# A two-block transformer on one core: the second block's prologues, attention order, weight slots and long-convolution loads, rearranged

## What is computed

```python
def second_block(x, c, ctx, ...):
    for layer in range(4):
        ...
        hx = rmsnorm(x, g_pre[layer]) * (1.0 + scale_x) + shift_x
        hc = rmsnorm(ctx, g_pre[layer]) * (1.0 + scale_c) + shift_c
        if kind == 0:
            yx, yc = mla_mixer(hx, hc, ...)
        elif kind == 1:
            yx, yc = swa_mixer(hx, hc, ...)
        else:
            yx, yc = hyena_mixer(hx, hc, ...)
        x = x + gate_x * rmsnorm(yx, g_post[layer])
        if with_ctx_out:
            ctx = ctx + gate_c * rmsnorm(yc, g_post[layer])
```

## Time and profile before

| | us |
|---|---|
| three runs, median (lowest to highest) | 3139.94 (3133.66 to 3140.37) |
| the profiled execution | 3137.42 |
| its span of instructions | 3135.6 |
| PE busy | 2908.2 (93%) |
| DVE busy | 1859.2 (59%) |
| ACT busy | 1151.2 (37%) |

### The profile page before, as it was taken

The page is one execution under the profiler, slowest core; times in us unless marked ns, Lnnn a source line. Parts: engine busy times, 40 slices in busy tenths (PEclk is TensorE's granted clock), DMA queues, the critical chain, the costliest instruction groups (busy, mean ns, idle before and its releaser), DMA issues.

```text
span 3135.6 us, 36002 instructions
## 1 busy us (share of the span) xinstructions
PE 2908.2 (93%) x14361; PEld 2337.9 (75%) x14361; DVE 1859.2 (59%) x3353; ACT 1151.2 (37%) x2022; POOL 94.2 (3%) x177
## 2 busy tenths in 40 slices
PE   7999889999999999999998888999998878989997
PEld 5767657778888887887787776888865556767885
DVE  5436677877676566663636566465436666455544
ACT  4224233232223444444534444443222110454443
POOL 0000000000000000000100000020000000000000
PEclk9999999999999999999999999999999998999999
DMA  6222115545554241103211110333331210321102
GB/s 236 88 88 91 52 59 201 201 175 181 169 168 134 94 141 61 58 24 101 81 50 31 31 31 4 128 116 101 106 92 34 64 53 25 125 77 58 41 18 94
DMA packets 109312, 288.77 MB, mean 92 GB/s; under 512 B 18326, under 2 KB 37815, under 8 KB 108888
## 3 DMA queue, kind: packets, MB, share of 16 engines
q1 hardware_dynamic: 97880, 249.05, 24.2%
q0 software_dynamic: 9392, 32.48, 2.8%
q10 hardware_dynamic: 1872, 4.93, 0.4%
HBM read 257.05 MB, written 24.12 MB: 90 GB/s over the span
## 4 chain that ended last, share of the span: by engine, by line
PE 81%; DVE 10%; ACT 5%; issue 1%; DMA 1%; SPq 1%; ACTq 0%; POOL 0%; DVEq 0%; POOLq 0%
PE ps L1826 19%; PE ps L1828 19%; PE ps L1827 19%; PE ps L2061 5%; PE ps L1859 2%; PE ps L2119 2%; PE ps L2093 2%; PE ps L2048 2%; ACT pt L2391 2%; PE ps L2135 1%; PE ps L1975 1%; PE ps L2082 1%; DVE tmp L2727 1%; PE ps L2016 1%; PE ps L2018 1%
## 5 line engine op out<-in xcount | busy, mean ns | idle before, releaser
L1826 PE MATMUL ps<-hh,whi 128*128 128x256 f32 (+1 forms) x2424 | 919.4, 379 | 24.6 <-DVE hl L2567 12.0
L1827 PE MATMUL ps<-hl,whi 128*128 128x256 f32 (+1 forms) x2424 | 871.8, 360 | 0.0
L1828 PE MATMUL ps<-hh,wlo 128*128 128x256 f32 (+1 forms) x2424 | 871.6, 360 | 0.0
L1826 PEld LDWEIGHTS ps<-hh,whi 128*128 128x128 f32 x2424 | 459.7, 190 | 130.6 <-issue 26.2
L1827 PEld LDWEIGHTS ps<-hl,whi 128*128 128x128 f32 x2424 | 460.5, 190 | 90.2 <-issue 21.2
L1828 PEld LDWEIGHTS ps<-hh,wlo 128*128 128x128 f32 x2424 | 459.0, 189 | 71.3
L2576 DVE TENSOR_TENSOR wlo<-raw,whi 128x1024 fp32r<-128x1024 f32 x249 | 303.9, 1222 | 243.8 <-ACT whi L2198 243.2
L2198 ACT ACTIVATE whi<-raw 128x1024 fp32r<-128x1024 f32 x249 | 262.4, 1055 | 300.9 <-PE ps L1828 274.5
L2061 PE MATMUL ps<-pt,v 128*128 128x256 f32 x768 | 215.8, 404 | 27.2 <-ACT pt L2391 16.1
L2391 ACT ACTIVATE pt<-ps 128x512 f32<-128x512 f32 (+1 forms) x200 | 109.5, 579 | 249.1 <-PE ps L2048 248.8
L2887 DVE TENSOR_REDUCE sm<-ps 128x1 f32<-128x768 f32 (+3 forms) x176 | 129.4, 735 | 93.1 <-PE ps L2018 48.4
(11 more groups left out here) (373 smaller groups left out, 4568.4 us busy)
## 6 DMA issues: line engine op xcount, KB each, us to landing
raw<-in_wall SPq DMA_DIRECT2D x249, 512.0 KB, 4.3
mb<-in_wmod SPq DMA_DIRECT2D x128, 512.0 KB, 3.6
xb<-xpark SPq DMA_DIRECT2D x24, 384.0 KB, 4.7
xpark<-F POOLq DMA_DIRECT2D x32, 256.0 KB, 2.3
upark<-tmp POOLq DMA_DIRECT2D x18, 384.0 KB, 2.7
u<-upark SPq DMA_DIRECT2D x24, 256.0 KB, 3.1
tmp<-tmp SPq DMA_DIRECT2D x80, 64.0 KB, 2.0
early<-in_wm SPq DMA_DIRECT2D x8, 512.0 KB, 6.4
```

The lines of the kernel that those rows point to most:

```text
L1826: e.matmul(out, L[0], R[0], start=start, stop=False)
L1827: e.matmul(out, L[0], R[1], start=False, stop=False)
L1828: return e.matmul(out, L[1], R[0], start=False, stop=stop)
```

## The change

The new code differs from the old in all of these places; the functions that are not named stay as they are. The first block is the same but for its end.

- **Layer 0**: `context_norm`, `square_sums` and `first_in` go. After the feed-forward network come `rms_stages` for the final norm, `final_gain`, the norm of all 768 columns (`layer_in`), and then three tiles together. Fourteen zero matmuls precede the first sums and 22 the first products.
- **MLA input**: the squares of the latents are taken in `latent_norm` itself, after the tiles before it are done, and the layout order of the weight blocks (`latent_tiles`) goes with `Two`.
- **Layer to layer**: `Two` holds three tiles on both sides instead of six, `XH`/`XL` and the slots' bookkeeping go, and 22 zeros stand before the first product of the next layer.
- **Attention**: the projections of the next head or tile are played in one go ahead of the present one's units, with banks by `take`; their evictions follow at once. Each row of scores claims two banks. One `bias` serves both rows. `rope` is four ACT copies of 32 partitions. SWA gets 17, 14 or 7 zeros ahead of a tile's first scores.
- **Long convolutions**: `load_u` moves from behind `conv_out` to the last frequency block of a transform, and the first inputs of the context line come behind four steps of the spectra.

```diff
-    XH, XL = (sb([P, NS, SLOT], F32R, x, sE) for x in ("xhi", "xlo"))
...
-    idle_before = {"out": 9, "head": 10}
+    idle_before = {2: 14, (11, NC_): 9, (12, NC_): 9, (13, NC_): 9, ("lat", 0, 0): 12, ("lat", 3, 0): 12, "out": 9, "head": 10,
+                   ("tile", True, 0): 17, ("tile", False, 0): 14, ("tile", False, 1): 7}
...
+    xf = [[(dve, ("ffn", 1, c))] for c in range(8)]
+    R = rms_stages(2, F, xf, NC_, T, D, KD)
+    for k in range(KD):
+        stage("final_gain", k, R, [R] if k == KD - 1 else [])
...
+        R = rms_stages(10 + l, F, tx, 0, T, D, KD)
+        h_done[l] = [(dve, ("H", 10 + l, KD - 1))]
+        return norm_stages(10 + l, tx, SEGS, (COEF[:, c + 8:c + 16], COEF[:, c:c + 8]),
+                           (MODC[:, c0:c0 + 8], MODX[:, c0:c0 + 8]), (dve, ("coef_in", l)), 0, R, (act, ("rstd", 10 + l)), hfree)
...
-        last = Two(6, 0, KD, H, src, src)
+        last = Two(3, KD, H, src, src, False)
...
         rest(0)
         bx = root(NC_, T)
-        stage("rstd", [root_of(NC_, T, bx)])
+        root_2(NC_, T, bx)
+        rest(1)
+        rest(2)
...
-                if u["w"] > 512:
-                    u["bk"].append((banks.claim(2 * s), banks.claim(2 * s + 1)))
-                else:
-                    u["bk"].append((banks.claim(2 * s + self.side[s]),))
-                    self.side[s] = 1 - self.side[s]
+                u["bk"].append((banks.claim(2 * s), banks.claim(2 * s + 1)))
                 stage("score", u, s, u["bk"][s], u["sm"])
-                stage("bias", u, s, u["sm"])
+            stage("bias", u, u["sm"])
...
-        play(tile_stages(KD, H, tH, gr, cq(3)))
-        squares = latent_squares(0, 4, gr)
-        play(tile_stages(KD, H, tH, SEGS, cq(4)))
-        latent_norm(0, 4, gr, 512, col("gq", 4 * j, 4), squares)
+        for c in (4, 5):
+            play(tile_stages(KD, H, tH, SEGS, cq(c)))
+        latent_norm(0, 4, gr, 512, col("gq", 4 * j, 4))
         play(tile_stages(KD, H, tH, SEGS, ev_kr))
-        latent_norm(4, 2, SEGS, 256, col("gkv", 2 * j, 2), squares)
+        latent_norm(4, 2, SEGS, 256, col("gkv", 2 * j, 2))
...
         for h in range(8):
+            if h + 1 < 8:
+                make_qk(h + 1)
+            if h % 2 and h < 6:
+                make_qr(h // 2 + 1)
+                make_v(h // 2 + 1)
             attend_head(h)
...
-        first = Two(6, 3, KD, H, sx, sc)
-        cross(before, l, first, evac, 6)
+        first = Two(3, KD, H, sx, sc, True, warm=[(None, 22)])
+        cross(before, l, first)
...
-                    if qt == 3 and tile < 7:
-                        make_q(tile + 1)
-                    if qt == 4 and tile % 2 == 0 and tile < 6:
-                        make_k(tile // 2 + 1)
...
         for tile in range(8):
+            if tile + 1 < 8:
+                make_q(tile + 1)
+            if tile % 2 == 0 and tile < 6:
+                make_k(tile // 2 + 1)
             attend_tile(tile)
...
                         stage("inverse", m, o, f - 1, seg, ib)
+                    if f == nt - 1:
+                        load_u(seg)
...
                     stage("z_out", l, m, a, n, q, s0)
                     ups[seg].drop(s0)
-                load_u(seg)
...
         stage("tables_in", 1)
         stage("tables_in", 0)
-        load_u(0)
...
         for _ in range(4):
             next(ahead)
+        load_u(0)
...
         def rope(g, b, src, cs, cs_mark, scale, swap, j, m, name):
-            wait_all(w, (pe, g), m)
-            A(TMP[:, m.i, 0:src.shape[1]], src, ACT.Copy).then_inc(*act.up(("rope", name), b))
+            n = src.shape[1]
+            wait_all(w, (pe, g), j)
+            for d, s, c in swap:
+                x = A(TMP[d:d + c, j.i, 0:n], src[s:s + c, :], ACT.Copy, scale=1.0 if scale is None else scale)
+            x.then_inc(*act.up(("rot", name)))
```

More of the change, by code:

```diff
@@ L291, in build_program @@
         tiles += [("long", 0), ("long", 1)] if x else [("short",)]
[L292 to L293 removed]
+    tiles += range(248, wall.shape[0])
+    wt = {"made": 0, "at": 0, "end": {}, "cap": len(tiles) - 1, "limit": len(tiles) - 1}
     plain, slot_free, last_h = set(), {}, []
[L297 removed]
     def block(tile, k, width=1):
         m = wt["at"] // 8
[L302 to L304 removed]
+        while wt["made"] <= min(m + AHEAD, wt["cap"]):
+            prepare()
         tile.blocks[k] = (m, (wt["at"] % 8) * P)
@@ L307, in block @@
         wt["at"] += width
[L309 to L327, removed]
-    def prepare(lows=True):
-        m = wt["made"]
-        if m not in plain:
-            s = next(x for x in slots if x[0] < NS or m < wt["six"])
-            slots.remove(s)
-            slot_of[m] = s
-        stage("weights", m)
+    def prepare(lows=True):
+        stage("weights", wt["made"])
         if lows:
-            stage("weights_lo", m)
+            stage("weights_lo", wt["made"])
         wt["made"] += 1
@@ L405, in step @@
             if k == 0:
-                g.banks = [banks.claim(i) for i in at] or [banks.take() for _ in range(tok // 2 if tok else len(groups))]
+                g.banks = [banks.take() for _ in range(tok // 2 if tok else len(groups))]
             block(g, k, 2 if tok else 1)
@@ L1027, in layer_out, with cross @@
         align()
-    def cross(before, l, first, leave, n):
+    def cross(before, l, first):
         tO, att_end = before
@@ L1058, in rest @@
             for k in range(KD):
-                last.context(i, k)
+                last.context(i, k, False)
         def root(a, b):
@@ L1274, in flush, with stacked @@
             self.multiply()
-    def stacked(g, i, dst, name, free, later, context=None):
+    def stacked(g, i, dst, name, free):
         a, b = g.groups[i]
@@ L1380, in mla @@
         tk = [(dve, ("half", l, 4 + k)) for k in range(2)]
-        wt["six"] = 0
-        free = [(dve, ("half", l, 6)), *att_free, *[(pe, ("w", m)) for m in slot_of if slot_of[m][0] >= NS]]
+        free = [(dve, ("half", l, 6)), *att_free]
         ptr = Ring(4)
@@ L1442, in attend_head @@
                               "ptfree": free, "vfree": v if h % 2 and end else None, "drops": [(vb, v)] if h % 2 and end else []})
-                    for _ in range(1 if with_ctx else 2 - i):
-                        next(between, None)
             qn.drop(b2["qn", h])
@@ L1792, in enter_3 @@
     def enter_3(gr, cq):
-        first = Two(3, 3, KD, H, *normed(3)[:2], False)
-        cross(before, 3, first, cq, 6)
+        first = Two(3, KD, H, *normed(3)[:2], True, warm=[(None, 22)])
+        cross(before, 3, first)
+        wt["cap"] = wt["limit"]
+        pump(3)
+        for c in range(3):
+            cq(c)(first.main_tiles[c])
         return normed(3)[2], None
```

611 lines of the change are left out of this document (175 added, 436 removed).

## The result

The new kernel takes 3357.63 us (3352.57 to 3358.74); the old one, run beside it on the same chip, 3140.15. The ratio is 1.069, 95% interval 1.067 to 1.071. The forecast was 3246 with a range of 3180 to 3335: right in direction, wrong in size. The change costs 217 us, twice the 106 of the sum.

A forecast was written before the change was run, and what follows sets the result against it. PE, busy 93% of the span, was taken as the bound, so each place was costed as PE time without a product; the terms summed to 106 us on 3137.4, giving 3246 against the runs' median, range 3180 to 3335.

The forecast's parts named there:

- the units stay PE's: MLA: 7.4 us of PE work in a 768-column unit against a softmax loop of 6.1, so PE's part is longer.
- +8 and +6: MLA of layers 0 and 3: uncovered units and waits behind `take` cost 8 and 6 us; ends 0 and 20 each.
- About 1 us: MLA: what the projections covered, the short context unit and a head's first unit, was about 1 us for each.
- DVE's modulation work: MLA of layer 0: this work ends before the stage in the new order and gives about half of 16 us back.
- +42: SWA: projections in front and the softmax loop cost 32 us, a lower clock 10 more; ends +10 and +90.
- +11.5, +11.5, +6.5: Three layer changes: 6.5 us each for lost cover, plus 5 at the first two for the context norm's wait.
- The chain gets shorter: Layer changes: three fewer DVE additions and a merged root save about 2 us, so 8.4 - 2 = 6.5 each.
- 5 us gap at the first context product: Layer changes: PE was to show a gap of about 5 us before the first context product.
- Layer 0's entry (+19): Between feed-forward network and first products: 31 us without products in the new order, less 12 before, costs 19 us.
- the latents (+6.5): MLA input: 12 zeros (2.8 us) and the last two sums' waits (3.7) cost 6.5 us, in layers 0 and 3.
- -8: Convolutions: moving the input loads frees waits for a filter's weights and a spectrum, 8 us gained; range -12 to +6.
- A cold PE in both kinds of attention: Rival: gaps lower PE's clock, all SWA units at 1.2 GHz and both MLA layers at +20: 3335 us; chance 0.23.

The follow-up runs named there:

- a_rows128: The new kernel with the remainder matmuls of all scores contracting 128 partitions again instead of 64: 3292.36 us, ratio 1.050 to the old kernel.
- b_swa_front: The old kernel with SWA's projections of the next tile played in one go in front of each tile, rotation still by DMAs: 3177.20 us, ratio 1.014.
- a_sum: The new kernel with 128-partition score remainders, no 22 zeros at the three layer changes, and the old order of squares and roots there: 3252.89 us, ratio 1.038.
- a_swa_cold: The new kernel with 128-partition score remainders and without the zeros ahead of a tile's first scores in SWA: 3294.56 us, ratio 1.050.

## Why the forecast was wrong, point by point

**The missing term: 61 us by the ratios.** The forecast went through the edits by name (order, banks, biases, rotation, zeros) and never through the matmuls' operands; "the units stay PE's" took PE's work as unchanged. It was the largest single cost of all: 17.0, 30.7 and 16.9 us in the new kernel's stretches, with 5.6 of the last a lower clock.

**MLA (+8 and +6; without the height 25.6 and 14.8).** Two steps failed. "About 1 us" for what the projections covered was 1.57 or more for the second unit alone, and the price stood in the old trace's last head. The waits behind `take`, put at 2 us for four heads, were 1.2 to 2.2 at six. Gross the gaps made 20.5 in layer 0 and not 16, and no row shows anything of the half that was credited to DVE's modulation work.

**SWA (+42; +49.4, of which 30.7 is the height).** The total looks right by two errors that cancel. The term for fronts and loop was 42 and is 18.7 in a_rows128. The loop did not grow as costed: with 128 partitions and ACT copies the new SWA, with its single bias, is 333.1 us against 331.2, although 16.8 us of products left it and 15.8 of zeros came. The eviction in front was sized well for DMAs (b_swa_front +43), but the change itself takes these DMAs away. The forecast costed the ACT copies, and what they spare only as an end of its range. (Its sum for that eviction is also off: the listed terms make 7.8 before any overlap, and it says 8.2 with it, some 3 us over seven tiles.) Its sign, some 375 us from first to last score, came true (357.1 and the 16.8 that were moved out), which shows that a total alone is a weak test.

**Layer changes (+11.5, +11.5, +6.5; measured 21.7, 19.4 and, less 8.1 for the latents, 21.2).** "The chain gets shorter" was the failed step. It took the root of the context as merged, where the new code splits a merged one, and didn't look at what is queued ahead of the residuals on DVE: 6 to 8 us. The 22 zeros were taken to pay for themselves; they cost 4.6 to 5.1. Without both, 9.8, 7.2 and 9.6 are left in a_sum. That these are near the forecast is in part luck, because its 5 us gap at the first context product did not come: at the first two changes PE waits 1.78 there, since the held stream starts so late that the context's norm is nearly done. At layer 3, where the forecast put no new gap, the wait behind the held stream grew from 4.67 to 10.42, in a_sum as well, and what ends it is a weight's remainder:

```profile
2956.75 0.77 PE L1564 MATMUL ps<-hh,whi 128*128 128x512 f32 x1 [10.42 <-DVE wlo L2298]
```

The chain there runs through the context's norm on DVE, then through three evictions and the rounding of the next weights on ACT, and their remainder on DVE. That is the late weights which the forecast named as its upper bound and didn't put into the sum.

**Layer 0's entry (+19) and the latents (+6.5).** The entry's mechanism was right as far as the timeline tells; no run takes this part of the change back. Before, PE had 5.9 us without products and not the 12 that were counted; after, 33.6 for a forecast of 31:

```profile
1042.88 3.22 PE L1575 MATMUL ps<-onesr,zeror 128*128 128x512 f32 x14
1045.94 7.03 PE L1594 MATMUL ps<-tmp,ones 128*128 128x512 f32 x16
1057.35 12.11 PE L1594 MATMUL ps<-tmp,ones 128*128 128x512 f32 x32 [4.38 <-ACT tmp L1891]
1069.11 5.16 PE L1575 MATMUL ps<-onesr,zeror 128*128 128x512 f32 x22
1076.67 0.38 PE L1564 MATMUL ps<-hh,whi 128*128 128x256 f32 x1 [2.40 <-DVE hl L2290]
```

So +27.7; the latents' sums, with the zeros and waits ahead of them, went from 7.0 to 15.4, +8.3. A gain was overlooked: the first score of MLA had waited for the key's eviction, and the next head's projections now cover that.

```profile
1212.41 0.76 PE L1826 MATMUL ps<-kn,hh 128*128 128x512 f32 x1 [4.30 <-DVE kn L2581]
```

27.7 + 8.3 - 4.3 makes 31.7, for the 31.2 of the table. The first block's -6.5 (forecast -3.4) is inside its spread: kernels with the old first block took 1041.6 to 1052.4 for it.

**The convolutions (-8; -3.9, and -5.3 alone).** Mechanism and sign were right. Of the two waits only the first was SP's doing; the 7.17, held by DVE's remainder, was not moved by freeing the queue.

**The rivals.** "A cold PE in both kinds of attention" gives 3335, close to the truth, and is not what happened: in MLA the clock was 0.98 and 0.96, and SWA's 0.92 is back at 0.95 once the height is. How the 30.7 of SWA divide between the changes of height and the clock that falls with them is not shown. Two runs give a hold: the same matmuls cost the old order 14.3 with no fall of the clock, and a fall from 0.95 to 0.92 in a_swa_cold, with the zeros gone, lengthened the stretch by 7.1.

## What to carry to other kernels

Read a diff for the shapes of its matmuls before its order: a cost that spreads the matmuls apart makes no wait, and only the starts in a timeline, or the mean of a group, show it. When cover is taken away, look in the old trace for the one place that already lacks it, and take the price from there at its full count. A total that fits is no proof of its terms; ask of each term for a row that only it can produce.

## What the runs showed of the chip

One change from matmuls of 128 partitions to ones of 64 and back costs 0.39 us at the full clock, whether one or two matmuls stand in between; over 96 rows of SWA and 80 of MLA it made 50 us on the old kernel and 61 on the new, where the granted clock fell with it. A cold start is cheap beside its cure: nine products at a clock of 0.50 lost some 2 us, 22 zeros ahead of them took 6.85. And through DMAs the same rotation made DVE wait 18.7 us in twelve steps when it was spread over other work, and 63.1 in nine when everything waited for it, 17 more than with ACT copies.
